# A two-layer transformer step: the last two experts of the second layer summed on TensorE, the gather of the other rows moved into the expert loop

## The chip, the cores and the metric

One core of a Trainium2 chip runs the whole step as one program. The metric is the time of one execution on the device, in microseconds (us). TensorE is called PE, VectorE DVE, ScalarE ACT, GpSimd POOL and SyncE SP. An engine's queue is where it issues DMAs.

## The reference, cut to what matters

288 tokens (256 of a prompt, 32 of a sample) of 1024 features pass two layers. A layer is an attention block with its layernorm, and then a mixture of 16 experts with a second layernorm, which is where the change lies. Each token goes to two experts, weighted by a gate:

```python
for e in range(N_EXPERTS):
    h = jax.nn.silu(t @ w_gate[e]) * (t @ w_up[e])
    y = y + gate[:, e:e + 1] * (h @ w_down[e])
...
x = layernorm(DN_ALPHA * x + ffn, p['ln2_g'][l], p['ln2_b'][l])
```

All arithmetic is float32. An expert has 2 x 1024 x 512 weights up and 512 x 1024 down, 6 MB; there are 16 in each layer.

## The kernel before, in words

Engines are programmed one by one and meet at semaphores. Tokens are held in three tiles (`TOKS`: 128, 128 and 32 rows), `x_tok[:, t, :]`.

*Routing* (`route`, line 1666, on DVE) gives each token two experts, two gates (`gates[:, s, t]`) and, for either, the row `64 * e + place` that its result will have (`row_ab`, and as an integer `out_row`). An expert takes 64 tokens at most (`CAP`); a flag says whether any has more, and behind the loop each engine loads that flag and branches over the code for the overflow (lines 968, 1371, 1782, 1930).

*Experts* go in the order of `expert_order` (line 400): up(e), then down(e - 1). `up` (PE, line 936) waits for the weights of the expert and multiplies 64 tokens by gate and up weights into bank 0 or 1. ACT makes the exponential (`gate`, line 1328), DVE the hidden rows (`form`, line 1756: four operations, the last with `h_ready`). `down` (PE, line 946) transposes them into bank 2, DVE copies them (`turned`, line 1765), and PE multiplies by the down weights into bank 3 or 4: features 0 to 511 for 64 rows in partitions 0 to 63, features 512 to 1023 in the others. ACT copies that bank to `y_out` and issues two stores to `y_dram` in DRAM (`store`, line 1333). SP issues the weight loads three experts ahead, each when its buffer is free (lines 524 to 530).

*Bringing back.* POOL loads the parameters of the second norm (`ln_load`, line 1909), waits until all stores of the layer have landed, and issues six indirect gathers (`bring_back`, line 1931), two rows of 4 KB per token, into `back`. DVE meanwhile scales x by ALPHA (line 1821). Per tile `combine` (line 1827) waits for the tile's two gathers, adds `back * gate` to x twice (line 1831), takes the statistics of two half rows (`ln_half`, line 1648) and joins them (`ln_stats`, line 1651), which also subtracts the mean and multiplies by the gain (line 1657). ACT takes the root (line 1304) and `ln_finish` (line 1659) finishes the norm. SP stores each tile of the second layer to the output (line 597).

On DVE, `own(...)` issues an instruction that counts on a semaphore; `step(...)` also waits for it.

Of the kernel before, what the change touches and what calls it, by code (L numbers as in the profile page):

```python
# [25 lines left out]
D = 1024  # L26
# [18 lines left out]
CAP = 64  # L45
# [3 lines left out]
ROWS = NE * CAP  # L49
ALPHA = (2 * DEPTH) ** 0.25  # L50
# [14 lines left out]
for _name, _n in (("ident", P), ("ones", P), ("tri", P), ("rotq", NT),  # L65
                  ("cost", 3 * 16), ("sint", 3 * 16), ("iota", CAP), ("rowbase", NE), ("tri4", EPG * EPG)):
    CONST[_name] = (_at, _n)
    _at += _n
CONST_W = _at

def shape_constants():
# [23 lines left out]
    put("iota", slice(None), np.arange(CAP))  # L95
# [9 lines left out]
def encoder_step(nc, ins, outs):  # L105
    ctx = ExitStack()
    with ctx:
# [4 lines left out]
        ARENA = 52900  # L112
# [106 lines left out]
        back = Region(gu_one_at).cut(2, 3, D)  # L219

# [16 lines left out]
        biased = zr.cut(48)  # L237
        gt = zr.cut(192)
        eq = zr.cut(192)
        rank = zr.cut(48)  # L240
# [19 lines left out]
        x_first = Region(y_at).cut(D)  # L260
        assert zr.at <= Z + 3 * D
# [45 lines left out]
        back_in = [sem(f"back_in{t}") for t in range(3)]  # L307
        OV = ("ov_w", "ov_xg", "ov_gu", "ov_sig", "ov_h", "ov_ht", "ov_htc", "ov_y", "ov_yc", "ov_st", "ov_dve")
# [88 lines left out]
        def stores(l, e):  # L397
            return l * NE // 2 + e // 2 + 1
# [224 lines left out]
        def _(pe):  # L623
# [311 lines left out]
            def experts(l):  # L935
# [10 lines left out]
                def down(e):  # L946
# [6 lines left out]
                    if at > 2:  # L953
                        pe.wait_ge(y_copied, at - 2)
# [12 lines left out]
                pe.wait_ge(starts_ready, l + 1)  # L967
                more = pe.value_load(flag[0:1, 0:1], min_val=0, max_val=1)
                with pe.If(more > 0):
                    o = ov[l]  # L970
                    with pe.Fori(0, NE) as e:
                        with pe.Fori(0, PASSES - 1) as q:
# [7 lines left out]
                            expert_down(0, dn[0]).then_inc(o["ov_y"], 1)  # L980

# [169 lines left out]
            experts(1)  # L1151


        @block.scalar
        def _(ac):
# [167 lines left out]
            def experts(l):  # L1323
# [9 lines left out]
                def store(e):  # L1333
# [6 lines left out]
                    ac.wait_ge(y_copied, at)  # L1340
                    for n in range(2):
                        ac.dma_start(y_dram[CAP * e:CAP * (e + 1), 512 * n:512 * n + 512],
                                     y_out[64 * n:64 * n + 64, j, :]).then_inc(y_stored[j], 16)

# [19 lines left out]
                for e in range(3, NE):  # L1364
# [3 lines left out]
                    store(e - 1)  # L1368
                store(NE - 1)
                ac.wait_ge(starts_ready, l + 1)  # L1370
                more = ac.value_load(flag[0:1, 0:1], min_val=0, max_val=1)
                with ac.If(more > 0):
                    o = ov[l]
                    for j in range(2):
                        ac.wait_ge(y_stored[j], 32 * stores(l, NE - 1))
# [57 lines left out]
        def _(ve):  # L1433
# [232 lines left out]
            def route(l):  # L1666
# [46 lines left out]
                for t, (a, n) in enumerate(TOKS):  # L1713
                    for e in range(2):
                        c = NE * t + e
                        own(ts(pick[0:n, t, CAP * e:CAP * (e + 1)], cst("iota")[0:n], counts[0:n, c:c + 1],
# [38 lines left out]
            def experts(l):  # L1755
# [12 lines left out]

                form(0)
# [23 lines left out]
            def after_attention(l):  # L1793
# [186 lines left out]
```

## Time and profile before

| what | us |
|---|---|
| runs before | 956.57, 947.65, 949.15 |
| their median | 949.15 |
| profiled execution, its own time | 951.2 |
| its span, first to last instruction | 949.4 |
| PE busy in the span | 796.8 (84%) |
| DVE busy in the span | 331.0 (35%) |
| ACT busy in the span | 185.2 (20%) |

Times in the rows are microseconds from the start of the span. A row of the timeline gives start, duration, engine, line, operation, output<-inputs and, in brackets, the idle time before it and what ended that. `arena` is the SBUF tensor that holds nearly everything, `bank` is PSUM, `expert_rows` is `y_dram`. The second layer's experts run from 690 us on.

### The profile page before, as it was taken

The numbers are of one execution on the slowest core, as the hardware profiler recorded it, in microseconds if no ns is written. First come the engines' busy times: TensorE is split into PE (matmuls) and PEld (weight loads), VectorE is DVE, ScalarE is ACT, GpSimd is POOL, SyncE is SP. The second block draws the span as 40 slices with busy tenths as digits, with TensorE's granted clock in tenths as the row PEclk, the third lists the DMA queues.
The fourth block names the chain that finished last, engine by engine and source line by source line (L and its number), as shares of the span: only waits on it lengthen the run. The fifth ranks groups of instructions, "written<-read, shape, count | busy, mean of one in ns | idle before, by whom it ended". The sixth has DMA issues, their size and how long they took to land.

```text
span 949.4 us, 9961 instructions
## 1 busy us (share of the span) xinstructions
PE 796.8 (84%) x3956; PEld 395.7 (42%) x3956; DVE 331.0 (35%) x729; ACT 185.2 (20%) x450; POOL 44.0 (5%) x58
## 2 busy tenths in 40 slices
PE   6998999989999978777899788979899997877650
PEld 3665777453433322222444566655444332222210
DVE  1034454453422322113540353463453331212128
ACT  1213333010311211110110144511013111101010
POOL 1021000002000000000200000000110000000010
PEclk9998999997999999999999997989899999999885
DMA  9633008656999999999694600580789999999943
GB/s 361 213 107 145 1 1 320 256 241 224 401 429 424 426 425 428 424 427 409 201 405 130 252 2 1 212 364 21 300 328 421 428 426 425 424 427 424 422 138 102
DMA packets 43872, 273.30 MB, mean 288 GB/s; under 512 B 6424, under 2 KB 11230, under 8 KB 26160
## 3 DMA queue, kind: packets, MB, share of 16 engines
q1 hardware_dynamic: 32032, 243.66, 62.3%
q0 software_dynamic: 5888, 19.95, 6.3%
q10 hardware_dynamic: 5904, 9.04, 2.7%
q8 instruction: 32, 0.52, 0.2%
q14 instruction: 16, 0.13, 0.0%
HBM read 253.88 MB, written 18.73 MB: 287 GB/s over the span
## 4 chain that ended last, share of the span: by engine, by line
PE 53%; DMA 25%; DVE 11%; SPq 6%; ACT 2%; issue 2%; ACTq 0%; POOL 0%; DVEq 0%; POOLq 0%
DMA arena<-in_expert_w_up 23%; PE bank L889 16%; PE bank L831 6%; PE bank L903 5%; PE bank L1123 4%; PE bank L818 3%; SPq L476 2%; PE bank L754 2%; PE bank L806 2%; PE bank L912 2%; PE bank L799 1%; DVE arena L1831 1%; PE bank L651 1%; PE bank L732 1%; DMA arena<-expert_rows,out_row 1%
## 5 line engine op out<-in xcount | busy, mean ns | idle before, releaser
L889 PE MATMUL bank<-arena 128*64 128x512 f32 x1024 | 240.3, 626 | 49.8 <-DMA arena<-in_expert_w_up 48.1
L889 PEld LDWEIGHTS bank<-arena 128*64 128x64 f32 x1024 | 77.1, 144 | 209.8 <-issue 147.9
L903 PE MATMUL bank<-arena 128*64 128x512 f32 x512 | 116.9, 598 | 16.6 <-DVE arena L1753 16.6
L1753 DVE COPY arena<-bank 128x256 f32<-128x256 f32 x32 | 13.6, 424 | 280.1 <-PE bank L896 280.1
L903 PEld LDWEIGHTS bank<-arena 128*64 128x64 f32 x512 | 33.9, 136 | 77.5 <-issue 54.8
L1317 ACT ACTIVATE arena<-bank 128x256 f32<-128x256 f32 x32 | 12.3, 383 | 267.1 <-PE bank L889 267.1
L1761 DVE RECIPROCAL arena<-arena 128x256 f32<-128x256 f32 x32 | 56.1, 1753 | 1.1
L831 PE MATMUL bank<-arena 128*128 128x512 f32 x128 | 56.0, 595 | 0.0
L1123 PE MATMUL bank<-arena 128*128 128x512 f32 x96 | 41.7, 594 | 3.6 <-DVE arena L1454 3.6
L818 PE MATMUL bank<-arena 128*128 128x288 f32 x128 | 37.9, 456 | 4.1 <-DVE arena L1860 4.1
L1339 ACT COPY arena<-bank 128x512 f32<-128x512 f32 x32 | 18.8, 586 | 98.7 <-PE bank L903 98.7
L1179 ACT COPY arena<-bank 128x512 f32<-128x512 f32 (+2 forms) x30 | 15.8, 537 | 106.9 <-PE bank L651 69.7
L831 PEld LDWEIGHTS bank<-arena 128*128 128x128 f32 x128 | 24.0, 190 | 29.6 <-issue 29.5
L996 PE MATMUL bank<-arena 128*128 128x512 f32 x64 | 31.4, 653 | 2.2 <-DMA arena<-in_w_mem_kv 1.2
L1321 ACT COPY arena<-arena 128x512 f32 x28 | 31.4, 1126 | 8.6 <-issue 7.8
L818 PEld LDWEIGHTS bank<-arena 128*128 128x128 f32 x128 | 27.0, 217 | 12.8 <-issue 5.0
L651 PE MATMUL bank<-arena 128*128 128x128 f32 (+1 forms) x144 | 22.5, 312 | 8.3 <-DVE arena L1875 3.2
L1454 DVE COPY arena<-bank 128x512 f32<-128x512 f32 (+3 forms) x20 | 12.8, 647 | 46.5 <-PE bank L996 16.3
L1123 PEld LDWEIGHTS bank<-arena 128*128 128x128 f32 x96 | 18.1, 190 | 25.9 <-issue 22.0
L1911 POOL DMA_DIRECT2D arena<-in_ln_g x4 | 2.3, 565 | 554.1 <-ACT arena L1321 312.8
L754 PE MATMUL bank<-arena 128*128 128x64 f32 (+1 forms) x172 | 26.1, 297 | 0.9 <-ACT arena L1273 0.7
L651 PEld LDWEIGHTS bank<-arena 128*128 128x128 f32 (+1 forms) x144 | 20.7, 201 | 13.3 <-DVE arena L1875 4.2
(250 smaller groups left out, 869.7 us busy)
## 6 DMA issues: line engine op xcount, KB each, us to landing
arena<-in_expert_w_gate SPq DMA_DIRECT2D x32, 2048.0 KB, 21.1
arena<-in_expert_w_up SPq DMA_DIRECT2D x32, 2048.0 KB, 26.2
arena<-in_expert_w_down SPq DMA_DIRECT2D x64, 1024.0 KB, 28.6
arena<-in_w_out SPq DMA_DIRECT2D x4, 2048.0 KB, 9.5
expert_rows<-arena ACTq DMA_DIRECT2D x64, 128.0 KB, 7.8
arena<-in_w_kv_shared SPq DMA_DIRECT2D x3, 2048.0 KB, 9.3
arena<-in_w_mem_kv SPq DMA_DIRECT2D x2, 2048.0 KB, 20.1
arena<-sorted_rows POOLq DMA_DIRECT2D x2, 2048.0 KB, 9.1
```

The lines of the kernel that those rows point to most:

```text
L476: sp.dma_start(g_kv, ins["kv_norm_g"][0].partition_broadcast(P)).then_inc(small_in, 16)
L651: last = tr(b[:, k * n:(k + 1) * n], src[0:n, t, k0 + k::KC], ident[0:n, 0:n])
L754: last = mm(b[:, qt * w:(qt + 1) * w], pt[:, P * i:P * i + P], v[:, kt, h * w:(h + 1) * w], start=(i, kt) == mine_[0], stop=(i, kt) == min ...
L806: last = mm(b[:, 0:NT], w_q[:, k, 4 * g + hh, :], cq_feat[:, k, :], start=k == 0, stop=k == 2)
L818: last = mm(b[:, 0:NT], w_inb[k // 4][:, k % 4, P * c:P * c + P], x_feat[:, k, :], start=k == 0, stop=k == KC - 1)
L831: last = mm(b[:, :], x_feat[:, k, P * t:P * t + P], w_out[k // 4][:, k % 4, 512 * c:512 * (c + 1)], start=k == 0, stop=k == KC - 1)
L889: last = mm(bank[j][64 * half:64 * half + 64, :].rearrange("p (u f) -> p u f", u=2), slots[:, k, 0:CAP], w[:, :, k, 256 * half:256 * half ...
L903: last = mm(bank[3 + j][64 * n:64 * n + 64, :], hid_t[:, j, c, 64 * half:64 * half + 64], w[:, half, c, 512 * n:512 * n + 512], start=(hal ...
L996: last = mm(b[:, :], feat[:, k, P * t:P * t + P], w[:, k, :], start=k == 0, stop=k == KC - 1)
L1123: last = mm(b[:, :], x_feat[:, k, P * t:P * (t + 1)], w_kvs[c][:, k, :], start=k == 0, stop=k == KC - 1)
L1321: return nc.scalar.copy(xg[:, j], xs[:, bass.ds(at, CAP), :].rearrange("p s k -> p k s"))
L1761: step(V.reciprocal(a, a))
```

## The change

`PAIR` switches it on for the second layer alone.

- Experts 14 and 15 are not stored. ACT copies their 64 rows from PSUM to `y_pair` (`keep`): partitions 0 to 63 for expert 14, 64 to 127 for expert 15. The gathers then need the stores of experts 0 to 13 only, and POOL issues them when those have landed.
- After expert 5's `form`, DVE makes from `row_ab` and `gates` a one-hot matrix per tile, tokens by the 128 rows of the pair, with the gates as its values (`pair_weights`). In the same place the entries of `out_row` that lie in experts 14 and 15 become row 0, with a gate of 0 (`pair_gate`). PE transposes the matrices after up(6) and loads the overflow flag there too; DVE copies them to `pair_t` after expert 7's `form`.
- x is scaled by ALPHA after `form` of expert 14, in both layers.
- Behind the loop DVE adds the gathered rows to x for all three tiles first. Per tile PE then sums in two banks x (by an identity matmul) and `pair_t` times `y_pair` (`add_tile`), and the statistics and the first step of the norm read those banks, in halves of 512 columns.

```diff
+PAIR = (False, True)
+PAIR_ROW = ROWS - 2 * CAP
...
+        y_pair = Region(gu_one_at + 6 * D).cut(2, 512)
...
-            return l * NE // 2 + e // 2 + 1
+            return sum(stored(m) for m in range(l)) + e // 2 + 1
+        def stored(l):
+            return NE // 2 - PAIR[l]
+        def copied(l, e):
+            return sum(2 * stored(m) for m in range(l)) + e + 1
+        def pairs(l):
+            return sum(PAIR[:l])
+        def sum_bank(t, c):
+            return bank[((0, 1), (5, 6), (2, 7))[t][c]]
...
-                    if at > 2:
-                        pe.wait_ge(y_copied, at - 2)
+                    if e > 1:
+                        pe.wait_ge(y_copied, copied(l, e - 2))
+                    elif l and PAIR[l - 1]:
+                        pe.wait_ge(pair_copied, 4 * pairs(l))
+                    elif l:
+                        pe.wait_ge(y_copied, copied(l - 1, NE - 2 + e))
...
+                    if PAIR[l] and (what, e) == ("up", 6):
+                        pe.wait_ge(pair_ready, pairs(l) + 1)
+                        for t, (a, n) in enumerate(TOKS):
+                            last = tr(bank[5][:, a:a + n], pair_hot[0:n, t, :], ident[0:n, 0:n])
+                        last.then_inc(pair_turned, 1)
+                        pe.wait_ge(starts_ready, l + 1)
+                        more = pe.value_load(flag[0:1, 0:1], min_val=0, max_val=1)
+                if not PAIR[l]:
+                    pe.wait_ge(starts_ready, l + 1)
+                    more = pe.value_load(flag[0:1, 0:1], min_val=0, max_val=1)
...
+            def add_tile(l, t):
+                a, n = TOKS[t]
+                pe.wait_ge(part_ready, 3 * pairs(l) + t + 1)
+                for c in range(2):
+                    mm(sum_bank(t, c)[0:n, :], ident[0:n, 0:n], x_tok[0:n, t, 512 * c:512 * c + 512], start=True, stop=False)
+                if t == 0:
+                    pe.wait_ge(pair_taken, pairs(l) + 1)
+                for c in range(2):
+                    if t == 0:
+                        pe.wait_ge(pair_copied, 4 * pairs(l) + 3 + c)
+                    last = mm(sum_bank(t, c)[0:n, :], pair_t[:, a:a + n], y_pair[:, c, :], start=False, stop=True)
+                last.then_inc(tile_ready, 1)
...
+                def keep(e):
+                    j, at = e % 2, NE * l + e + 1
+                    ac.wait_ge(down_done, at)
+                    for n in range(2):
+                        nc.scalar.copy(y_pair[64 * j:64 * j + 64, n, :],
+                                       bank[3 + j][64 * n:64 * n + 64, :]).then_inc(pair_copied, 1)
...
-                    store(e - 1)
-                store(NE - 1)
+                    (keep if PAIR[l] and e == NE - 1 else store)(e - 1)
+                (keep if PAIR[l] else store)(NE - 1)
...
+                def pair_weights():
+                    own(ts(pair_row, row_ab, float(-PAIR_ROW), None, ALU.add))
+                    step(ts(pair_keep, row_ab, float(PAIR_ROW), None, ALU.is_ge))
+                    step(stt(pair_keep, row_ab, float(ROWS), pair_keep, ALU.is_lt, ALU.mult))
+                    step(ts(pair_keep, pair_keep, -1.0, 1.0, ALU.mult, ALU.add))
+                    own(tt(row_ab, row_ab, pair_keep, ALU.mult))
+                    step(tt(pair_gate, gates, pair_keep, ALU.mult))
+                    own(V.tensor_copy(out_row[:, :], row_ab[:, :, :].rearrange("p s t -> p (s t)")))
+                    for t, (a, n) in enumerate(TOKS):
+                        own(ts(pair_hot[0:n, t, :], cst("iota")[0:n], pair_row[0:n, 0, t:t + 1], gates[0:n, 0, t:t + 1],
+                               ALU.is_equal, ALU.mult))
+                        step(ts(pair_tmp[0:n], cst("iota")[0:n], pair_row[0:n, 1, t:t + 1], gates[0:n, 1, t:t + 1],
+                                ALU.is_equal, ALU.mult))
+                        step(tt(pair_hot[0:n, t, :], pair_hot[0:n, t, :], pair_tmp[0:n], ALU.add),
+                             pair_ready if t == 2 else None)
...
+                    if PAIR[l] and e == 5:
+                        pair_weights()
+                    if PAIR[l] and e == 7:
+                        ve.wait_ge(pair_turned, pairs(l) + 1)
+                        own(V.tensor_copy(pair_t, bank[5][:, 0:NT]), pair_taken)
+                    if e == NE - 2:
+                        ve.wait_ge(x_sorted, 96 * (l + 1))
+                        for t in range(3):
+                            own(ts(x_tok[:, t, :], x_tok[:, t, :], ALPHA, None, ALU.mult))
...
-                ve.wait_ge(x_sorted, 96 * (l + 1))
-                for t in range(3):
-                    own(ts(x_tok[:, t, :], x_tok[:, t, :], ALPHA, None, ALU.mult))
...
+                    if PAIR[l]:
+                        ve.wait_ge(tile_ready, 3 * pairs(l) + t + 1)
+                        sums = [sum_bank(t, c)[0:n, :] for c in range(2)]
+                        for c in range(2):
+                            own(V.bn_stats(bn[0:n, t, 6 * c:6 * c + 6], sums[c]))
+                        own.settle()
+                        step(V.bn_aggr(mean_var[0:n, t, :], bn[0:n, t, :]), var_ready)
+                        ve.wait_ge(ln_in, 32 * (2 * l + 2))
+                        for c in range(2):
+                            own(stt(x_tok[0:n, t, 512 * c:512 * c + 512], sums[c], mean_var[0:n, t, 0:1],
+                                    ln2_par[0:n, 0, 512 * c:512 * c + 512], ALU.subtract, ALU.mult))
+                        return
...
+                if PAIR[l]:
+                    for t in range(3):
+                        n = TOKS[t][1]
+                        ve.wait_ge(back_in[t], 32 * (l + 1))
+                        for s in range(2):
+                            step(stt(x_tok[0:n, t, :], back[0:n, s, t, :], pair_gate[0:n, s, t:t + 1], x_tok[0:n, t, :],
+                                     ALU.mult, ALU.add), part_ready if s else None)
...
+                if PAIR[l]:
+                    po.wait_ge(pair_ready, pairs(l) + 1)
...
-                        po.wait_ge(y_stored[j], 32 * stores(l, NE - 1))
+                        po.wait_ge(y_stored[j], 32 * stores(l, 2 * stored(l) - 1))
```

The table of constants grows by 64 columns (`iota` to 128).

## Rows read from the trace of the kernel before

**Rows 1.** The chain that ended last, in order of time: start us, us, what held it.
```profile
632.90 13.93 PE bank L831 x32
...
897.36 9.03 PE bank L889 x32
...
911.94 3.68 PE bank L903 x16
916.82 2.39 DMA expert_rows<-arena
...
920.00 1.00 POOL arena L1936
921.30 5.19 DMA arena<-expert_rows,out_row
...
945.76 1.28 DVE arena L1664
```

**Rows 2.** Busy by stage: us; engines' busy us (x instructions); PEclk, DMA share, GB/s.
```profile
768.00:802.00 34.00, 26.75 (x122) 8.63 (x118) 9.65 (x15) 6.30 (x9) 0.00 (x0) 1.00 1.01 424
897.40:906.40 9.00, 9.00 (x33) 2.69 (x33) 0.00 (x0) 0.00 (x0) 0.00 (x0) 0.78 0.94 388
906.40:916.00 9.60, 8.16 (x36) 2.66 (x36) 5.54 (x9) 1.27 (x3) 0.00 (x0) 1.00 0.13 29
```

**Rows 3.** Timeline of DVE from 898 us on.
```profile
906.86 0.42 DVE L1753 COPY arena<-bank 128x256 f32<-128x256 f32 x1 [16.55 <-PE bank L896]
...
912.34 1.90 DVE L1821 TENSOR_SCALAR arena<-arena 128x1024 f32<-128x1024 f32 x3 [0.45 <-issue]
926.59 2.60 DVE L1831 SCALAR_TENSOR_TENSOR arena<-arena 128x1024 f32<-128x1024 f32 x2 [12.35 <-DMA arena<-expert_rows,out_row]
929.23 1.29 DVE L1649 BATCH_NORM_STATS2 arena<-arena 128x6 f32<-128x512 f32 x2
```

**Rows 4.** Timeline of ACT's queue, 891 to 893 us.
```profile
891.85 1.12 ACTq L1342 DMA_DIRECT2D expert_rows<-arena  x2
```

**Rows 5.** DMA issues, 891 to 893 us: KB each, us from issue to landing.
```profile
expert_rows<-arena ACTq DMA_DIRECT2D x2, 128.0 KB, 6.9
```

**Rows 6.** All stores of expert rows (line 1342), issue to landing.
```profile
DMA to landing us min/median/max: 2.3/7.8/10.8
```

**Rows 7.** Timeline of POOL, the sixth gather of the second layer.
```profile
926.26 0.85 POOL L1936 DMA_INDIRECT arena<-expert_rows,out_row  x1 [0.30 <-issue]
```

**Rows 8.** All gathers of expert rows (line 1936), issue to landing.
```profile
DMA to landing us min/median/max: 4.3/5.3/7.1
```

**Rows 9.** Timeline of POOL, 874 to 876 us.
```profile
874.72 0.56 POOL L1911 DMA_DIRECT2D arena<-in_ln_g  x1 [158.38 <-ACT arena L1321]
```

**Rows 10.** DMA issues, 874 to 876 us.
```profile
arena<-in_ln_b POOLq DMA_DIRECT2D x1, 512.0 KB, 13.7
```

**Rows 11.** Groups of DVE instructions by shape: busy us, mean ns, idle before.
```profile
L1649 DVE BATCH_NORM_STATS2 arena<-arena 128x6 f32<-128x512 f32 x24 | 15.9, 689 | 0.6
...
L1552 DVE TENSOR_REDUCE arena<-bank 128x1 f32<-128x256 f32 x28 | 11.0, 416 | 7.4 <-PE bank L678 7.4
...
L1810 DVE SCALAR_TENSOR_TENSOR arena<-arena,bank 128x512 f32<-128x512 f32 x8 | 5.5, 687 | 30.4 <-PE bank L831 30.4
...
L1561 DVE TENSOR_REDUCE arena<-arena 128x2 f32<-128x256 f32 x6 | 2.5, 420 | 0.2
...
L1716 DVE TENSOR_SCALAR arena<-arena 128x64 f32<-128x64 f32 x8 | 2.0, 310 | 0.1
```

**Rows 12.** Groups of ACT instructions by shape.
```profile
L1339 ACT COPY arena<-bank 128x512 f32<-128x512 f32 x32 | 18.8, 586 | 98.7 <-PE bank L903 98.7
```

**Rows 13.** Timeline around experts 5 to 8, second layer.
```profile
760.43 0.42 DVE L1763 TENSOR_TENSOR arena<-arena,bank 128x256 f32<-128x256 f32 x1
...
768.46 0.50 PE L896 MATMUL bank<-arena 128*128 128x128 f32 x2
...
787.09 7.09 PE L889 MATMUL bank<-arena 128*64 128x512 f32 x32 [2.48 <-DMA arena<-in_expert_w_up]
```

More of the change, by code:

```diff
@@ L65 @@
 for _name, _n in (("ident", P), ("ones", P), ("tri", P), ("rotq", NT),
-                  ("cost", 3 * 16), ("sint", 3 * 16), ("iota", CAP), ("rowbase", NE), ("tri4", EPG * EPG)):
+                  ("cost", 3 * 16), ("sint", 3 * 16), ("iota", 2 * CAP), ("rowbase", NE), ("tri4", EPG * EPG)):
     CONST[_name] = (_at, _n)
@@ L94, in shape_constants @@
     put("sint", slice(None), st.transpose(1, 0, 2).reshape(P, -1))
-    put("iota", slice(None), np.arange(CAP))
+    put("iota", slice(None), np.arange(2 * CAP))
     put("rowbase", slice(None), np.arange(NE) * CAP)
@@ L109, in sem @@
             return ctx.enter_context(nc.semaphore(name))
-        ARENA = 52900
+        ARENA = 53000
         arena = ctx.enter_context(nc.sbuf_tensor("arena", [P, ARENA], F32))
@@ L237, in encoder_step @@
         biased = zr.cut(48)
+        pair_hot = Region(zr.at).cut(3, 2 * CAP)
         gt = zr.cut(192)
         eq = zr.cut(192)
+        pair_tmp = Region(zr.at).cut(2 * CAP)
         rank = zr.cut(48)
@@ L260, in encoder_step @@
         x_first = Region(y_at).cut(D)
+        pair_t = zr.cut(NT)
+        pair_row = zr.cut(2, 3)
+        pair_keep = zr.cut(2, 3)
+        pair_gate = zr.cut(2, 3)
         assert zr.at <= Z + 3 * D
@@ L307, in encoder_step @@
         back_in = [sem(f"back_in{t}") for t in range(3)]
+        pair_ready = sem("pair_ready"); pair_turned = sem("pair_turned"); pair_taken = sem("pair_taken")
+        pair_copied = sem("pair_copied"); part_ready = sem("part_ready"); tile_ready = sem("tile_ready")
         OV = ("ov_w", "ov_xg", "ov_gu", "ov_sig", "ov_h", "ov_ht", "ov_htc", "ov_y", "ov_yc", "ov_st", "ov_dve")
@@ L1151, in _ @@
             experts(1)
+            for t in range(3):
+                add_tile(1, t)
         @block.scalar
@@ L1339, in store @@
                     nc.scalar.copy(y_out[:, j, :], bank[3 + j][:, :]).then_inc(y_copied, 1)
-                    ac.wait_ge(y_copied, at)
+                    ac.wait_ge(y_copied, copied(l, e))
                     for n in range(2):
@@ L1374, in experts @@
                     for j in range(2):
-                        ac.wait_ge(y_stored[j], 32 * stores(l, NE - 1))
+                        ac.wait_ge(y_stored[j], 32 * stores(l, 2 * stored(l) - 1))
                     with ac.Fori(0, NE) as e:
@@ L1715, in route @@
                         c = NE * t + e
-                        own(ts(pick[0:n, t, CAP * e:CAP * (e + 1)], cst("iota")[0:n], counts[0:n, c:c + 1],
+                        own(ts(pick[0:n, t, CAP * e:CAP * (e + 1)], cst("iota")[0:n, 0:CAP], counts[0:n, c:c + 1],
                                sel_any[0:n, c:c + 1], ALU.is_equal, ALU.mult), pick_ready if (t, e) == (2, 1) else None)
@@ L1817, in after_attention @@
                 experts(l)
-                ve.wait_ge(x_sorted, 96 * (l + 1))
-                for t in range(3):
-                    own(ts(x_tok[:, t, :], x_tok[:, t, :], ALPHA, None, ALU.mult))
                 own.settle()
-                if l == 0:
+                if l == 0 and not PAIR[0]:
                     copies("memx1", mem_dst(mem_feat1))
@@ L1835, in combine @@
                     ln_stats(2 * l + 1, t)
+                if PAIR[l]:
+                    for t in range(3):
+                        n = TOKS[t][1]
[3 more added lines that the diff above has]
+                                     ALU.mult, ALU.add), part_ready if s else None)
                 combine(0)
```

2 lines of the change are left out of this document (removed).

## The prediction

> **What bounds the kernel now.** I read the chain of waits first, from its end. The reader is to see two stretches. Through the second layer's experts each step is released by a load of expert weights, down to the load that lets expert 15's up projection start at 897.36 [rows 1]. The stage table shows why: in 768 to 802 us the DMA engines are busy for all of the stretch at 424 GB/s, while PE is busy for 26.75 of 34 us [rows 2]. After 897.36 nothing streams that is not already on its way (0.94 of the engines' time up to 906.4, 0.13 behind it [rows 2]), and the chain becomes serial: down(14), down(15) ending at 911.94 + 3.68 = 915.62, the last store of expert rows to DRAM, the wait of GpSimd for it, six indirect gathers, then VectorE alone to 945.76 + 1.28 = 947.04 [rows 1]. The span ends 2.36 us after that, with the last output. DVE stands idle for 12.35 us before 926.59, for the gathered rows [rows 3]. So the stage that the change touches is bound by a round trip through DRAM (store, landing, gather) and then by DVE's sum and norm of three tiles.
>
> **The change, part by part.**
>
> *The gather moves forward.* It needs the stores of experts 0 to 13 only. Expert 13's rows are issued from 891.85 on ACT's queue and take 6.9 us to land [rows 4, 5]: about 899.3 for the second of them (issued some 0.55 us after the first). The landings of all such stores lie between 2.3 and 10.8 [rows 6], so 894.7 to 903.2. Before, GpSimd's first gather began 920.00 - (916.82 + 2.39) = 0.79 after the landing [rows 1]; so it begins at 900.1 (latest 904.0). Six issues took 926.26 - 920.00 = 6.26 us to the start of the last [rows 1, 7]: the last starts at 906.4 (910.3). A gather lands 4.3 to 7.1 us after its issue, median 5.3 [rows 8]: tile 0's second gather (issued at 901.4) by 906.7, tile 2's last by 911.7.
>
> These landings were seen on an idle DMA; now the tail of the weight stream runs beside them until about 907 (0.94 busy to 906.4, 0.13 from there to 916 [rows 2]). What GpSimd's queue gets beside the stream is shown by its two norm loads, issued from 874.72 on: 1.05 MB in 0.54 + 13.7 = 14.2 us, 74 GB/s [rows 9, 10]. At that pace the gather moves 0.45 MB until 907, the stream ends a microsecond later, and the remaining 1.9 MB of 2.36 (288 tokens, two rows of 4 KB) follow at the bare pace, which tile 0 showed: 1.05 MB in the 5.19 us after its second issue [rows 1], 0.2 MB a us with a landing's own delay in it. Tile 0 then lands at about 911, tile 2 by 917.5 at the latest. I take these later landings. They are asked for at 912.34, 914.98 and 917.62 (below), so the cost is 0, bounds 0 to 2.8 us (worked out under the first of the other cases). That the last weights come a microsecond later costs nothing: down(15) wants them at 911.94, the stream is over at 908.
>
> *VectorE's sum starts earlier.* DVE is in order: its first multiply-add stands behind the last copy of the hidden rows, and in the profile its next instruction after that copy starts at 912.34 [rows 3]. That was the scaling of x (three operations, 1.90 us), which moves to after expert 14's hidden form, where DVE is idle 16.55 us before 906.86 [rows 3]; both layers move it, and in the first it lay behind a gather too: cost 0. Left in place it would cost 1.90 here. So the first multiply-add moves from 926.59 to 912.34: 14.25 us gained. Behind it stand the same six multiply-adds and three norms, in another order: six first, 3 x 2.64 = 7.92 us (926.59 to 929.23 for a pair [rows 3]), to 920.26; then the norms.
>
> *The norm reads PSUM.* Per tile two statistics of 512 columns from PSUM instead of SBUF, and one 1024-column multiply split in two of 512. The trace has no statistics from PSUM. It has reductions of 256 columns from both: 420 ns from SBUF, 416 from PSUM, and a scalar-tensor-tensor of 512 columns from PSUM at 687 against 689 for the statistics from SBUF [rows 11]. So the source costs nothing that can be seen; the split costs one more fixed part, 2 x 0.69 against 1.28 for one over the whole row [rows 1, 11]: 0.1 per tile, 0.3 in all. Bounds: 0 (the two overlap fully) and 0.7 (two such costs per tile). The Trainium skill says otherwise (page "VectorE: DVE Perf Modes", section on the TRN2 errata): a VectorE operation has 120 fixed cycles from PSUM against 58 from SBUF. By that, my estimate would be 12 operations x 62 cycles / 0.96 GHz = 0.8 us more, 936.2 instead of 935.4; the two reductions above disagree with it, and the measurement decides.
>
> *Experts 14 and 15 by PE.* Removed: their two copies and four stores with the 2.39 us landing [rows 1]. Added on ACT: four copies of 64x512; by columns each is as the 128x512 one, 586 ns [rows 12]. The last two run from 915.7 to 916.9. Added on PE: twelve matmuls of 512 columns, 13.93 / 32 = 0.435 us each [rows 1]. Tile 0's two identity matmuls run while ACT copies (915.62 to 916.5; their x is summed at 914.98), its pair matmuls end at about 917.5. DVE asks for them at 920.26: 2.8 us of cover. At half the clock (0.87 each) tile 0 is ready at 919.1, still in time; tiles 1 and 2 are asked for 4 us apart and take 1.75. PE's branch over the overflow code stands before them, its register now loaded much earlier; DVE's load and branch took 0.45 [rows 3], also under the cover. Cost 0, and if the cover went, each microsecond past 2.8 costs one.
>
> *Weights and transposes at experts 5 to 7.* Sixteen small DVE operations follow expert 5's form, which ends at 760.85 [rows 13]. The dearest like them, one-hot rows of 64 columns, take 310 ns [rows 11]; 6 x 0.38 (128 columns) + 10 x 0.31 = 5.4 us, done at 766.3. Behind them waits the copy of expert 5's turned rows, whose transposes start at 768.46 [rows 13]: covered by 2.2 us. PE waits for them at 768.46 as well, then does three transposes (0.25 each by the same row) and a register load, 0.5 by DVE's: 1.3 us before down(5), and down(5) and up(7) are that much later. PE then had 2.48 us of waiting for weights at 787.09 [rows 13], and the DMA engines have no gap there [rows 2], so loads issued a microsecond later lose nothing: 0, bounds 0 to 1.3. The constants are 32 KB longer, 0.1 us at the start at that rate; GpSimd's new wait is over 100 us before its gather.
>
> **The sum.** -14.25 + 0.3 + 0.1 = -13.85. The profiled execution took 951.2 (949.4 of span and 1.8 around it): 937.35. It lies 2.05 over the median of the three runs, 949.15; against that, 935.3, rounded up to 935.4 for small hand-overs.
>
> **The other ways it could go.**
>
> *The gather lands after VectorE asks for it.* For it: all six multiply-adds stand before the first norm, so tile 2's last row now holds up everything; the stream is still on; and the tokens of experts 14 and 15 all read row 0 instead. Against: 74 GB/s beside a stream that is about over. Place: the first multiply-add or tile 2's. If the gather moves nothing until 907 and then needs as long as an idle one at its slowest, 6.26 + 7.1 = 13.4 us, tile 2 is in at 920.4 instead of 917.62: 2.8 more, 938.2. With the slowest store (issue at 904.0 and the last at 910.3), 917.4: nothing. Chance 0.12, with a tail beyond 939.7.
>
> *PE's sums become the wait.* Tile 0's sum is ready after 920.26. For it: PE follows ACT's two copies, in series. Against: 2.8 us of cover. If copies took twice as long and PE ran at half the clock with 0.45 for the branch: copies to 918.1, both pair matmuls behind it to 919.9, still in time; another 2 us would give 937. Chance 0.03.
>
> *The gather crawls, and the kernel is slower.* One mechanism: the gather keeps the pace of the norm loads, 74 GB/s, to its end, because repeated reads of row 0 queue up where the stream did before. Then 2.36 MB take 32 us from 900.1, tile 2 is in at 932.0, and 2.61 + 12.9 us of sum and norms end at 947.5 instead of 947.04: 949.6. It decides from a last landing at 931.5 on; at half that pace it would be 1% slower and more. Against it: after the stream the rows of before show gathers landing in 7.1 at most [rows 8]. Chance 0.03.
>
> **How the numbers follow.** The forecast has 0.82. Its own scatter is that of the runs (947.65 to 956.57 before) and of 0 to 0.7 for the norm: 933 to 937.5. The late gather extends it to 941; the low end is 932.5, where the median falls by 2 as single runs do (947.65 lies 1.5 under theirs) and hand-overs cost nothing. About 1% is what a measurement of this kernel tells from no change, 939.7 to 958.6: faster 0.93 (forecast, PE's sums, most of the late gather), within 1% 0.05 (the rest of it and most of the crawl), slower 0.02.
>
> **What would show it.** Right: expert 15's up projection starts within a microsecond of 897.4; the gathers start at about 900 and end at 907; DVE's first multiply-add starts at 912 to 913 without waiting, six in a row to 920.3, and the first statistics follow without a gap; statistics from PSUM at 0.69; last DVE instruction at 933. Wrong: idle time of DVE before any of the six, named for gathered rows (late gather); idle time before the first statistics, named for PE (sums late); statistics or half-row multiplies at over 0.75 (PSUM dearer); expert 7 to 15 later than before by more than a microsecond (the transposes were not covered).

## The result, and the profile after

The changed kernel took 942.30, 941.67, 933.33 and 942.40 us: a median of 941.98. The kernel before, run beside it, had a median of 948.40 (946.92 to 956.57). The comparison gives a ratio of 0.986, with an interval of 0.9813 to 0.9906; the two medians alone would give 0.993, and the repeats below settle which is nearer (0.9845 and 0.9869). The forecast was 935.4 from 949.15, a ratio of 0.9855. So the kernel became faster by about as much as forecast, but the time itself lies 1 us above the upper end of the range (941.0). In two of the later sets one execution of a changed kernel was slow, 1054.98 and 1188.06 us at mean granted clocks of 0.74 and 0.65, and is left out of every median and ratio here.

The profiled execution took 942.3 us (span 940.5) against 951.2 before: 8.9 less. Two places make up that difference. I call *tail* the time from the start of expert 15's up projection to the end of DVE's last instruction. Here is the chain of waits of the changed kernel, to set beside [rows 1].

```profile
861.01 41.12 DMA arena<-in_expert_w_up
902.18 8.78 PE bank L916 x32
911.91 3.65 PE bank L930 x16
917.35 1.30 DVE arena L1939
918.67 1.30 DVE arena L1939
...
923.94 1.28 DVE arena L1939
925.25 1.31 DVE arena L1918 x2
926.82 1.41 DVE arena L1923 x2
928.34 1.29 DVE arena L1727
...
936.87 1.28 DVE arena L1727
```

The store, its landing, POOL and the gather are gone from the chain: DVE's first multiply-add follows the down projection, and everything behind it is DVE. The tail is 936.87 + 1.28 - 902.18 = 35.97 us; before it was 945.76 + 1.28 - 897.36 = 49.68 [rows 1]: 13.71 less, where the sum said 13.85. But expert 15 starts at 902.18 instead of 897.36, 4.82 later. 13.71 - 4.82 = 8.89 is the difference of the two executions. What those 4.82 are is the question that the experiments start from.

Inside the tail, the timeline of the changed kernel from 902 us on shows each engine:

```profile
902.18 8.78 PE L916 MATMUL bank<-arena 128*64 128x512 f32 x32 [4.36 <-DMA arena<-in_expert_w_up]
...
907.10 0.99 POOL L2043 DMA_INDIRECT arena<-expert_rows,out_row  x1 [26.30 <-DMA expert_rows<-arena]
...
913.37 0.86 POOL L2043 DMA_INDIRECT arena<-expert_rows,out_row  x1 [0.30 <-issue]
...
917.35 7.86 DVE L1939 SCALAR_TENSOR_TENSOR arena<-arena 128x1024 f32<-128x1024 f32 x6 [0.88 <-issue]
...
920.11 1.98 PE L1026 MATMUL bank<-arena 128*128 128x512 f32 x4
920.22 1.19 ACT L1405 COPY arena<-bank 64x512 f32<-64x512 f32 x2 [3.42 <-PE bank L930]
...
921.93 1.88 PE L1032 MATMUL bank<-arena 128*128 128x512 f32 x4
...
925.25 1.30 DVE L1918 BATCH_NORM_STATS2 arena<-bank 128x6 f32<-128x512 f32 x2
```

The six multiply-adds run in a row and wait only for issue (0.88 us), where DVE waited 12.35 us for gathered rows [rows 3]. From the start of expert 15 to the first multiply-add it was 926.59 - 897.36 = 29.23 us and is 917.35 - 902.18 = 15.17: 14.06 gained. From there to DVE's end it was 20.45 and is 20.80: 0.35 given back. The gather starts at 907.10, 4.92 us behind expert 15's start, and its last issue is at 913.37.

The stages of the changed kernel (us; busy us of PE, PEld, DVE, ACT and POOL; PEclk, DMA share, GB/s), to set beside [rows 2]:

```profile
902.20:911.00 8.80, 8.80 (x33) 2.70 (x34) 0.00 (x0) 0.00 (x0) 2.98 (x4) 0.81 1.02 419
911.00:920.00 9.00, 7.97 (x36) 2.64 (x36) 6.22 (x9) 1.54 (x3) 2.62 (x3) 1.00 0.73 264
920.00:938.20 18.20, 10.90 (x26) 3.66 (x24) 17.70 (x25) 3.32 (x6) 0.00 (x0) 0.87 0.15 59
```

The gather's transfers now lie beside the end of the weight stream: 264 GB/s in a stretch like the one that had 29 before. In the last stretch DVE is busy for 17.70 of 18.20 us: DVE bounds the end of the tail.

The gathers of the second layer (line 2043) from issue to landing. Where the gather is early, the profile gives a landing for tile 2's two gathers alone, while [rows 8] has all twelve of both layers; tile 2's two took 5.3 us each there.

```profile
DMA to landing us min/median/max: 5.7/5.9/6.1
```

So from the first issue to the last landing the six gathers took 913.37 + 6.1 - 907.10 = 12.4 us; before it was 926.26 + 5.3 - 920.00 = 11.6 [rows 1, 7].

The groups of DVE and ACT by shape from 905 us on, beside [rows 11, 12]:

```profile
L1923 DVE SCALAR_TENSOR_TENSOR arena<-bank,arena 128x512 f32<-128x512 f32 x4 | 2.8, 746 | 0.1
L1918 DVE BATCH_NORM_STATS2 arena<-bank 128x6 f32<-128x512 f32 x4 | 2.6, 689 | 0.0
...
L1405 ACT COPY arena<-bank 64x512 f32<-64x512 f32 x4 | 2.3, 580 | 7.7 <-PE bank L930 7.6
```

Statistics from PSUM take 689 ns, to the nanosecond what they took from SBUF [rows 11].

### The profile page after: what moved, and what is told of

Read it like the earlier page. It is cut to its first block, busy times and chain, and to the rows that moved or that the text cites. A ratio compares the mean times of both kernels' runs of the same rounds, so it can differ in the third digit from the quotient of the medians.

```text
span 940.5 us, 10036 instructions
## 1 busy us (share of the span) xinstructions
PE 807.9 (86%) x3983; PEld 402.1 (43%) x3983; DVE 335.1 (36%) x749; ACT 186.5 (20%) x452; POOL 44.1 (5%) x58
## 4 chain that ended last, share of the span: by engine, by line
PE 53%; DMA 26%; DVE 9%; SPq 6%; ACT 2%; issue 2%; POOL 0%; ACTq 0%; DVEq 0%; POOLq 0%
DMA arena<-in_expert_w_up 24%; PE bank L916 16%; PE bank L858 6%; PE bank L930 5%; PE bank L1176 5%; PE bank L845 3%; SPq L503 2%; PE bank L781 2%; PE bank L833 2%; PE bank L939 1%; PE bank L826 1%; PE bank L678 1%; PE bank L759 1%; PE bank L1141 1%; SPq L499 1%
## 5 line engine op out<-in xcount | busy, mean ns | idle before, releaser
L1816 DVE COPY arena<-bank 128x256 f32<-128x256 f32 x32 | 13.6, 424 | 274.7 <-PE bank L923 274.7
L1372 ACT ACTIVATE arena<-bank 128x256 f32<-128x256 f32 x32 | 12.3, 384 | 268.8 <-PE bank L916 268.8
L858 PEld LDWEIGHTS bank<-arena 128*128 128x128 f32 x128 | 24.0, 190 | 29.6 <-issue 29.5
L845 PEld LDWEIGHTS bank<-arena 128*128 128x128 f32 x128 | 27.8, 223 | 13.1 <-issue 5.0
L1176 PEld LDWEIGHTS bank<-arena 128*128 128x128 f32 x96 | 19.2, 202 | 29.3 <-issue 23.9
## 6 DMA issues: line engine op xcount, KB each, us to landing
arena<-in_expert_w_gate SPq DMA_DIRECT2D x32, 2048.0 KB, 22.5
```

The lines of the kernel that those rows point to most:

```text
L845: last = mm(b[:, 0:NT], w_inb[k // 4][:, k % 4, P * c:P * c + P], x_feat[:, k, :], start=k == 0, stop=k == KC - 1)
L858: last = mm(b[:, :], x_feat[:, k, P * t:P * t + P], w_out[k // 4][:, k % 4, 512 * c:512 * (c + 1)], start=k == 0, stop=k == KC - 1)
L1176: last = mm(b[:, :], x_feat[:, k, P * t:P * (t + 1)], w_kvs[c][:, k, :], start=k == 0, stop=k == KC - 1)
```

## The experiments

Theory A: the change does in its own stage what was forecast, and what lies ahead of the tail is scatter that both kernels have. Rival B: the change itself costs time ahead of its stage; B1 blames the scaling of x, which moved in the first layer too. Besides these, four terms of the sum are tested: that the early gather is the gain, PE's cover, the reads of row 0, and that DVE alone bounds the end. All ratios are against the kernel before, run in the same set.

**Both kernels again.** No edit.

> The changed kernel as it is. Its tail (start of expert 15's up projection to the end of the last DVE instruction) came out at 36.0 us against 49.7 before, as forecast, but that projection started at 902.2 instead of 897.4, and the lag is there before the second layer's experts begin (first up projection at 695.7 instead of 690.8). Theory A, the clock that TensorE is granted between the two layers differs from execution to execution whatever the change: runs spread from 933 to 942, and a new profile has the first up projection of the second layer anywhere in 690 to 697, the tail again 36.0. Theory B, the change itself makes the stretch slower: every run within 2 us of 942 and the first up projection at 695.7 again. The run at 933.33 speaks for A.

> The kernel before, unchanged, for a second profile. Five profiles of the changed kernel and its variants have expert 15's up projection of the second layer at 902.0 to 904.6, the one profile of before at 897.4. Theory A (the lag is scatter that both kernels have, by the clock and the start of the load stream): here it starts at 900 or later and the span is 952 or more, with the tail again 49.7 from that projection's start to the end of the last DVE instruction. Theory B (the change adds 5 us ahead of the tail): 897 to 898 again.

> The same kernel once more, a third profile of before. Theory A: anywhere in 897 to 906, not the same as the first two to within 1 us. Theory B: 897 to 898.

The changed kernel: 940.61, ratio 0.9845 (0.9794 to 0.9896). The kernel before, one execution each: 953.57 and 954.72. The landmarks of the profiles (us; the projection is that of keys and values at the start of the second layer, tile 0):

| profile | PE idle before the projection, and its time | second layer's first up | expert 15's up | tail |
|---|---|---|---|---|
| before | 2.77, 20.84 | 690.75 | 897.36 | 49.68 |
| before, again | 5.17, 23.39 | 693.14 | 899.54 | 49.86 |
| before, a third time | 4.44, 23.67 | 694.25 | 900.73 | 49.77 |
| changed | 4.21, 23.81 | 695.73 | 902.18 | 35.97 |
| changed, again | 1.82, 20.84 | 697.94 | 904.62 | 36.15 |
| changed, a third time (below) | 4.63, 23.69 | 697.47 | 903.52 | 36.48 |

The tail repeats within about 0.5 us for either kernel, the way to it moves by several for both. In the first pair of profiles the whole 4.82 us were there when the second layer's experts began (695.73 - 690.75 = 4.98); from there to expert 15 both kernels need the same, 206.61 and 206.45 us. And 2.97 of them are one group of instructions. The timeline of PE, in the kernel before as first profiled:

```profile
476.16 20.84 PE L1123 MATMUL bank<-arena 128*128 128x512 f32 x48 [2.77 <-DVE arena L1454]
```

the kernel before, again:

```profile
475.28 23.39 PE L1123 MATMUL bank<-arena 128*128 128x512 f32 x48 [5.17 <-DMA arena<-in_w_kv_shared]
```

the changed kernel as first profiled:

```profile
477.05 23.81 PE L1176 MATMUL bank<-arena 128*128 128x512 f32 x48 [4.21 <-DMA arena<-in_w_kv_shared]
```

and the changed kernel, again:

```profile
482.29 20.84 PE L1176 MATMUL bank<-arena 128*128 128x512 f32 x48 [1.82 <-DVE arena L1517]
```

The same 48 passes (a pass is one matmul instruction of the trace) take 20.84 or over 23 us, in both kernels. In the twelve profiles of this study they took 20.84 in seven, where PE had idled 1.11 to 2.77 us before them, and 22.5 to 23.8 in five, where it had idled 3.35 to 5.17. The granted clock over these stretches shows what differs (us; busy us of PE, PEld, DVE, ACT and POOL; PEclk, DMA share, GB/s). The kernel before as first profiled:

```profile
476.16:497.00 20.84, 20.84 (x50) 9.36 (x51) 8.64 (x11) 0.88 (x2) 0.00 (x0) 1.00 1.03 408
```

The changed kernel as first profiled, in two parts:

```profile
477.05:483.00 5.95, 5.95 (x7) 2.49 (x8) 5.81 (x7) 0.30 (x1) 0.00 (x0) 0.50 1.05 386
483.00:500.86 17.86, 17.86 (x44) 7.95 (x43) 2.66 (x5) 0.59 (x1) 0.00 (x0) 1.00 1.02 412
```

The short projection ran at 1.00 (2.4 GHz) throughout, and so it did in all seven; the long one began at 0.50 (1.2 GHz), and the five have means of 0.87 to 0.92. So the first profile of before was one with the short projection and the first of the changed kernel one with the long one: these 2.97 us are theory A's. The rest is not one thing: the changed kernel, again, had the short projection and still the latest experts, since its projection began only at 482.29.

Theory B's places did not come: 697.94 for 695.7, 899.54 and 900.73 for 897 to 898, and executions from 933.87 to 944.91 for all within 2 us of 942. Theory A's were missed by little (697.94 for 690 to 697, 899.54 for 900 or later, in a span of 951.8 for 952). One thing still speaks for B: all three profiles of the changed kernel start expert 15 later than all three of before. Against it, two variants below that have the changed kernel's code up to the second layer's experts start it at 898.73 (PE held up) and 898.07 (own rows). They ran in one set and on one chip with the second and third profile of before, which start it at 899.54 and 900.73: there the change costs nothing ahead of its stage.

**The scaling of x back behind the loop, in the first layer alone.**

```diff
-                    if e == NE - 2:
+                    if PAIR[l] and e == NE - 2:
...
+                if not PAIR[l]:
+                    ve.wait_ge(x_sorted, 96 * (l + 1))
+                    for t in range(3):
+                        own(ts(x_tok[:, t, :], x_tok[:, t, :], ALPHA, None, ALU.mult))
```

> The changed kernel with x of the first layer scaled behind the loop again, as before; the second layer as changed. Theory B1, the earlier scaling in the first layer is what slows the stretch between the layers (it is the only thing the change does there): the shared key and value projection of tile 0 takes 20.8 us as before, not 23.8, the first up projection starts near 691 and the median is 935 to 938. Theory A: no difference from the changed kernel beyond its own spread.

938.69, ratio 0.9852 (0.9807 to 0.9897): no difference from the changed kernel as it is, in the same set. The projection took 20.84 here, but so it did in the changed kernel as it is, in the same set, and over 23 in two profiles of before, which never had the scaling moved: B1 falls. This profile shows the one wait for gathered rows among the eight with an early gather, in the timeline of DVE:

```profile
919.02 2.61 DVE L1943 SCALAR_TENSOR_TENSOR arena<-arena 128x1024 f32<-128x1024 f32 x2 [0.88 <-issue]
922.13 5.22 DVE L1943 SCALAR_TENSOR_TENSOR arena<-arena 128x1024 f32<-128x1024 f32 x4 [0.50 <-DMA arena<-expert_rows,out_row]
```

0.50 us of waiting for tile 1's rows, with a gather that began 6.55 us behind expert 15's start instead of 4.92. The late start alone does not make the wait: in the changed kernel, again, it was 6.97 and nothing waited. Here tile 1's second gather took long as well, in the chain of waits:

```profile
914.26 7.79 DMA arena<-expert_rows,out_row
```

**Four more matmuls (eight passes) at the start of the second layer, ahead of the projection, so that PE idles less.** Nobody reads their result.

```diff
+                if t == 0:
+                    keep_warm(bank[1], 2048)
```

> The changed kernel with four idle matmuls of 512 columns (identity by constants into a bank that nobody reads) after the transposes of tile 0 between the layers, where PE stood idle 4.2 us before the key and value projection. Theory A's mechanism, the projection runs its first part at the low clock because PE idled before it: projection of tile 0 in 20.8 us in place of 23.8, and 3 to 4 us off those runs that were at 942; runs at 933 stay. Rival, the projection is held by its weights and not by the clock: no change, or up to 1 us slower where the idle matmuls outlast the wait.

940.27, ratio 0.9866 (0.9821 to 0.9911). The projection took 20.84 after 1.11 us of idling, but it started at 477.42, no earlier than elsewhere, since weights held it; no gain can be seen in the time (the changed kernel as it is: 940.61), and the 3 to 4 us expected did not come. The granted clock was 1.00 here, as in the six other profiles with 20.84, so the run does not show that the extra matmuls kept it there.

**The gather late again: POOL waits for ACT's copies of experts 14 and 15, all else as changed.**

```diff
+                    if PAIR[l]:
+                        po.wait_ge(pair_copied, 4 * (pairs(l) + 1))
```

> The changed kernel, but GpSimd's gathers of the second layer also wait until both copies of expert 15 are in y_pair. My theory, the early gather carries the gain: DVE's first multiply-add stands 11.4 us later (copies end, 0.8 to the first gather, 6.5 to tile 0's landing), the tail grows from 36.0 to 47.4 us and the time by 11 us. Rival, the gain is from the four stores and their landing that went: the tail stays within 2 us of 36.0 (the gathers would still be hidden by something).

956.10, ratio 1.0016 (0.9981 to 1.0051): the whole gain is gone. The timeline of POOL and DVE:

```profile
922.54 0.99 POOL L2043 DMA_INDIRECT arena<-expert_rows,out_row  x1 [41.96 <-ACT arena L1405]
...
929.27 2.60 DVE L1939 SCALAR_TENSOR_TENSOR arena<-arena 128x1024 f32<-128x1024 f32 x2 [12.49 <-DMA arena<-expert_rows,out_row]
...
931.93 3.78 PE L1026 MATMUL bank<-arena 128*128 128x512 f32 x4 [11.44 <-DVE arena L1939]
...
933.86 5.22 DVE L1939 SCALAR_TENSOR_TENSOR arena<-arena 128x1024 f32<-128x1024 f32 x4 [1.99 <-DMA arena<-expert_rows,out_row]
```

The 12.49 us of waiting are those of [rows 3] again (12.35). The tail is 50.0, 14.0 more than changed and 2.6 more than expected. 1.99 of that is a second wait: with all multiply-adds ahead of the first norm, nothing stands between tile 0's and tile 1's to cover the later gather, while in the kernel before tile 0's norm did. The four stores and their landing are gone in this run too: its first gather starts 922.54 - 902.02 = 20.5 us behind expert 15's start, against 22.6 before [rows 1], and the second wait takes those 2.1 us back. So the early start of the gather is the gain, and neither the removed stores nor the new order are worth anything without it. PE shows one thing more: after 11.44 us of idling its four identity passes took 3.78 us at a granted clock of 0.50 (1.2 GHz), against 1.98 at 1.00 (2.4 GHz) in the changed kernel.

**PE held up by four matmuls (eight passes) ahead of the sums.** Nobody reads their result.

```diff
+            keep_warm(bank[7], 2048)
             for t in range(3):
                 add_tile(1, t)
```

> The changed kernel with four idle matmuls of 512 columns (eight passes at 0.43, 3.4 us) on PE between the last down projection and the sums. The prediction put PE's sum of tile 0 2.8 us ahead of DVE's request; by the profile it is 1.4 us ahead, because a float32 matmul is two passes. With 1.4 of cover the first statistics wait on PE and the tail grows by 2.0 us, from 36.0 to 38.0; with 2.8 it grows by 0.6. If PE had no part in the end at all: 36.0.

940.46, ratio 0.9849 (0.9796 to 0.9901); the tail is 38.09, 2.1 longer. The timeline:

```profile
913.90 7.86 DVE L1940 SCALAR_TENSOR_TENSOR arena<-arena 128x1024 f32<-128x1024 f32 x6 [0.88 <-issue]
...
916.66 3.70 PE L685 MATMUL bank<-arena 128*128 128x512 f32 x8
...
921.92 1.88 PE L1032 MATMUL bank<-arena 128*128 128x512 f32 x4
...
923.90 1.30 DVE L1919 BATCH_NORM_STATS2 arena<-bank 128x6 f32<-128x512 f32 x2 [2.14 <-PE bank L1032]
```

Tile 0's sum is ready 923.80 - 898.73 = 25.07 us behind expert 15's start instead of 21.63, 3.44 later, and the tail is 2.12 longer: a cover of about 1.4 us (1.3 by this run, 1.44 by the profile of the changed kernel), and what went past it came out whole. One size of delay was tried.

**The gather reads the tokens' own rows instead of row 0.** Those of experts 14 and 15 hold something else by then and go in with a gate of 0; the sum is the same.

```diff
-                    own(tt(row_ab, row_ab, pair_keep, ALU.mult))
...
-                    own(V.tensor_copy(out_row[:, :], row_ab[:, :, :].rearrange("p s t -> p (s t)")))
```

> The changed kernel without the masking of the gathered rows: out_row keeps the rows of experts 14 and 15, which hold the first layer's results and are added with a gate of 0, so that the sum is the same. My theory, a repeated row costs the gather nothing: first gather to DVE's last wait as before, landings of 5 to 11 us, tail 36.0, time as the changed kernel within its scatter. Rival (the third of the other cases, reads of row 0 queue up): landings shorter by a microsecond or more.

939.06, ratio 0.9836 (0.9791 to 0.9881), tail 35.96. Tile 2's two gathers of the second layer from issue to landing:

```profile
DMA to landing us min/median/max: 6.6/6.9/7.2
```

With row 0 they took 5.7 and 6.1 in the changed kernel as first profiled, and 4.7 to 7.5 over the seven profiles that read it. The longer landings go with an earlier start of the gather, that is with more of the weight stream beside it, and not with the rows: here it began 3.76 us behind expert 15's start, and the two profiles with row 0 that began at 3.37 had 7.1 to 7.5. The rival wanted shorter landings than with row 0; they are not shorter. Reading one row many times costs nothing that shows.

**The last step of the norm off DVE, for tiles 0 and 1.** ACT multiplies by the reciprocal of the root, POOL adds the last parameter; DVE goes on to the next tile, and SP's stores of these tiles wait for POOL.

```diff
+                if n == 3 and t < 2:
+                    own.settle()
+                    step(V.reciprocal(rstd[:, t, :], rstd[:, t, :]), rstd_ready)
+                    return
...
+                    if l == 1 and t < 2:
+                        ac.wait_ge(rstd_ready, t + 1)
+                        nc.scalar.mul(x_tok[:, t, :], x_tok[:, t, :], rstd[:, t, :]).then_inc(scaled, 1)
...
+            for t in range(2):
+                po.wait_ge(scaled, t + 1)
+                G.tensor_tensor(x_tok[:, t, :], x_tok[:, t, :], ln2_par[:, 1, :], ALU.add).then_inc(shifted, 1)
```

> The changed kernel with the last step of the norm of tiles 0 and 1 (x times rstd plus the shift, 1.28 us on DVE each) taken from DVE: ACT multiplies, GpSimd adds. Since DVE is busy without a gap from its first multiply-add to the end, and the norms start 1.4 us behind PE's sums, both steps should come off the end: the tail shrinks from 36.0 by 2.4 to 33.6 us, if ACT (about 1.1 us) and GpSimd are done with tile 1 in the 4.2 us that DVE needs for tile 2. Rival: GpSimd's addition of 1024 columns takes over 3 us or holds DVE up, and the tail stays at 36 or grows. In the time 2.4 us of 940 is less than its scatter shows.

> The changed kernel once more, beside the one above on the same chip. Scatter as theory A has it: a profile with the tail at 36.0 us and expert 15's up projection anywhere in 897 to 905; median 938 to 943 where before is at 952 to 956.

940.16, ratio 0.9841 (0.9814 to 0.9867), and the changed kernel as it is, beside it, 943.32, ratio 0.9869 (0.9843 to 0.9896). The medians differ by 3 us, the intervals overlap. The timeline:

```profile
917.19 7.86 DVE L1947 SCALAR_TENSOR_TENSOR arena<-arena 128x1024 f32<-128x1024 f32 x6 [0.89 <-issue]
...
929.60 2.35 POOL L2069 TENSOR_TENSOR arena<-arena 128x1024 f32<-128x1024 f32 x1 [17.51 <-ACT arena L1477]
...
931.66 1.15 ACT L1477 ACTIVATE arena<-arena 128x1024 f32<-128x1024 f32 x1 [1.42 <-DVE arena L1731]
...
932.89 2.34 POOL L2069 TENSOR_TENSOR arena<-arena 128x1024 f32<-128x1024 f32 x1 [0.94 <-ACT arena L1477]
...
934.71 1.60 DVE L1735 SCALAR_TENSOR_TENSOR arena<-arena 128x1024 f32<-128x1024 f32 x1
```

From the first multiply-add to DVE's end: 934.71 + 1.60 - 917.19 = 19.12 instead of 20.80, 1.7 less (a gain of 2.4 was expected). A tile takes 3.28 us of DVE instead of 4.29; 0.3 went into the last operation, which took 1.60 instead of 1.28 while POOL's addition ran until 935.23. The end of the tail is indeed DVE's, and this version has the shortest tail of the study, 936.31 - 901.58 = 34.73 us, though the time doesn't tell it from the changed kernel. The changed kernel as it is missed its expectation by a little: 943.32 for 938 to 943, and a tail of 36.48 for 36.0.

## Why the prediction was right, and where it was wrong

*The mechanism and its size held.* The tail fell by 13.71 us, and over three profiles of each kernel from 49.77 to 36.20, 13.6, against 13.85. With the gather late the gain was gone. In the timed sets the changed kernel as it is was 954.27 - 940.61 = 13.7 and 955.07 - 943.32 = 11.8 us faster, the variants that leave the tail as it is 14 to 16. The medians of the first comparison, of four executions each, were only 948.40 - 941.98 = 6.4 apart, so that its ratio agrees with the forecast to 0.0005 is partly luck. The interval of the last set, 0.9843 to 0.9896 of 955, is 10 to 15 us, so the 13.7 of the tail lie within it; that a microsecond or two is lost ahead of the tail it does not exclude, and that stays open.

*The step that failed is the base.* "It lies 2.05 over the median of the three runs, 949.15; against that, 935.3" took three runs for the level of the kernel before, and the forecast's own range of 933 to 937.5 was half as wide as those runs (947.65 to 956.57); only the late gather stretched it to 941. In the later sets the kernel before had medians of 954.27, 955.29 and 955.07, within 947.42 to 958.79. 954.3 - 13.85 = 940.4 is what this step should have given: the sets of the changed kernel gave 941.98, 940.61 and 943.32. The scatter was to be seen beforehand, since one of the three runs had 956.57; that scatter lies ahead of the tail, so it belongs at full width on the new time. The signs given as places in the span (expert 15 at 897.4, the first multiply-add at 912 to 913, DVE's end at 933) came about 5 us late for the same reason: 902.18, 917.35 and 938.15. One profile of before could not show where it comes from. The projection after PE's idle time, 20.84 us at the full clock or up to 23.8 with a start at half, is one place of it, worth 3 us; the others stay open.

*VectorE's sum.* First multiply-add 15.17 us after expert 15's start, forecast 912.34 - 897.36 = 14.98. The idle time before it, in which DVE loads the overflow flag and branches, was 0.88 instead of the 0.45 of [rows 3], and the copy before it came 0.25 earlier. Why it is longer was not tried; the run with own rows had 0.52.

*The norm from PSUM.* +0.35 where 0.3 was the sum: 746 ns for a half-row multiply, two of them 1.41 us against 1.28 for one over the row [rows 1]. Each takes 746 instead of the 687 of [rows 11], but the two overlap; the 687 has one input in PSUM too, so the 59 ns between them are not PSUM's, and what they are was not tried. The Trainium skill (page "VectorE: DVE Perf Modes", section on the TRN2 errata), with its 120 fixed cycles against 58, put 0.8 us on it by the estimate in the prediction. The statistics show no difference between the two sources, 689 ns for both, and the measurement decides.

*The gather.* It was to begin at 900.1, 2.74 us behind expert 15's start, and began at 4.92 (3.37 to 6.97 over the eight profiles with an early gather): in the first profile the store of expert 13 was issued at 898.54, nearer to expert 15 than in [rows 4], and landed in 6.7 us as forecast (6.9 [rows 5]). Its pace was mis-sized the other way. The sum had tile 2 in 917.5 - 900.1 = 17.4 us after the first issue; it took 12.4, and 11.0 to 13.8 over the eight profiles, against 11.1 to 12.3 in the three of before and the one with the gather late. The 74 GB/s of the norm loads were the wrong row (and from 900.1 to 907 they are 0.51 MB, not 0.45; nothing hung on it). The two errors went opposite ways: tile 2 was in at 919.5 and asked for at 922.63, a cover of 3.2 us where the sum had left 0.1. Of the eight profiles one waited, 0.50 us, for tile 1's rows. The bound of 2.8 was not reached.

*PE's sums.* A float32 matmul of 512 columns shows in the trace as two passes, 0.43 us apart; the 32 instructions of [rows 1] are 16 such matmuls, and the sum took them for 32. The groups of PE from 915 us on:

```profile
L1026 PE MATMUL bank<-arena 128*128 128x512 f32 x8 | 3.9, 605 | 0.0
...
L1032 PE MATMUL bank<-arena 128*128 128x512 f32 x8 | 3.8, 592 | 0.0
```

Eight instructions stand there for two tiles of two matmuls each. Tile 0's sum is ready at 921.93 + 1.88 = 923.81 and asked for at 925.25: a cover of 1.4 us, not 2.8. It cost nothing here, and the run with PE held up shows where it would have.

*Weights and transposes.* The timeline of the changed kernel around expert 6, to set beside [rows 13]:

```profile
765.76 0.16 DVE L1834 TENSOR_SCALAR arena<-arena 128x6 f32<-128x6 f32 x1
...
769.34 0.28 DVE L1846 TENSOR_TENSOR arena<-arena 32x128 f32<-32x128 f32 x1
...
773.45 0.61 PE L1001 MATMUL bank<-arena 128*128 128x128 f32 x3
...
792.07 7.09 PE L916 MATMUL bank<-arena 128*64 128x512 f32 x32 [1.87 <-DMA arena<-in_expert_w_up]
```

DVE needed 3.9 us instead of 5.4 (nine of the sixteen operations, not six, are 128 columns wide, at 0.28 to 0.34 each; the other seven took 0.16 to 0.17, not 0.31) and was done 3.8 us before PE's transposes, which took 0.61. PE's next wait for weights is 1.87 instead of 2.48: 0.6 us of the slack went, where 1.3 was forecast. From the second layer's first up to expert 15's up the profiles of before took 206.4 to 206.6 us, the changed kernel 206.45, 206.68 and 206.05: the cost is 0, as taken. Three variants took 207.7, 209.0 and 211.4; in the last two the chain goes through the landing of the sorted rows at the layer's start (21.95 us from 696.47 on in the run with the scaling back), ahead of any instruction of the change in this layer. Why it is late there was not tried.

*The other ways.* The late gather came once, at 0.50 us; PE's sums never became the wait by themselves; the crawl did not come, and the run with own rows gives no sign of its reason, the repeated row 0.

## What to carry to other kernels

Judge a change at the end of a kernel by the length of its own stage, from the last thing it leaves alone to the last instruction: here that repeated within about 0.5 us where the whole time scattered by more than ten. Add the gain to a level of the kernel before that has more than three runs in it, or give the time a range as wide as theirs. And when the sums of all tiles are put ahead of the first norm, the last gather gates them all; with a late gather that order cost a second wait of 1.99 us here.

## What the runs showed of the hardware that was not expected

- The six gathers of the second layer, 2.36 MB, were in 11.0 to 13.8 us after their first issue beside the end of a weight stream (419 GB/s in all in 902.2 to 911 us), and in 11.1 to 12.3 with no stream beside them; the norm loads, 1.05 MB in the middle of the stream, took 14.2 [rows 9, 10]. What a queue gets beside a stream could not be carried from one kind of transfer to the other.
- The same 48 passes of PE took 20.84 us at a granted clock of 1.00 (2.4 GHz), after idle times of 1.11 to 2.77, and 22.5 to 23.8 at means of 0.87 to 0.92, after 3.35 to 5.17; four passes took 3.78 at 0.50 (1.2 GHz) after 11.44, against 1.98 at 1.00.
- DVE's last step of the norm, for the last tile, took 1.60 us beside POOL's addition, against 1.28 alone. The Trainium skill (page "SBUF — State Buffer", section "Who interferes with whom") says that a DVE instruction with two SBUF inputs contends with a GpSimd instruction that reads SBUF; the 0.32 more, in an overlap of 0.52 us (934.71 to 935.23), fit it. One instruction shows it, and no run tried it apart.
